# A two-layer encoder trunk on one core: splits of the dense mixer one turn earlier, another order and form of the router, another hand-over at the end

## The reference

```python
def swiglu(h, w_gate_up, w_down):
    g, u = jnp.split(h @ w_gate_up, 2, axis=-1)
    return (jax.nn.silu(g) * u) @ w_down

def moe_swiglu(h, w_router, w_gate_up, w_down):
    ...
    logits = (t @ w_router).astype(jnp.float32)
    top_val, top_idx = lax.top_k(logits, TOP_K)
    gates = jax.nn.softmax(top_val, axis=-1)
    combine = jnp.sum(jax.nn.one_hot(top_idx, N_EXPERTS, dtype=jnp.float32) * gates[..., None], axis=1)
    y = jnp.zeros_like(t)
    for e in range(N_EXPERTS):
        y = y + combine[:, e:e + 1].astype(t.dtype) * swiglu(t, w_gate_up[e], w_down[e])
    return y.reshape(B, S, D)

# in reference(), per layer l
        x = x + jnp.concatenate([y_self, y_mem], axis=-1) @ w_out[l]
        h = rmsnorm(x, ffn_norm_g[l])
        if l % 2 == 0:
            x = x + swiglu(h, w_gate_up_dense[l // 2], w_down_dense[l // 2])
        else:
            x = x + moe_swiglu(h, w_router[l // 2], w_gate_up_moe[l // 2], w_down_moe[l // 2])
    ...
    return rmsnorm(x, final_norm_g)
```

## Time and profile before

| | us |
|---|---|
| median of 3 runs | 1471.72 |
| lowest and highest | 1469.70, 1471.96 |
| profiled execution, its time | 1471.91 |
| profiled execution, its span | 1470.0 |
| PE busy | 1424.3 (97%) |
| DVE busy | 1156.0 (79%) |
| ACT busy | 949.9 (65%) |
| POOL busy | 40.0 (3%) |

### The profile page before, as it was taken

The page is one execution under the profiler, slowest core; times in us unless marked ns, Lnnn a source line. Parts: engine busy times, 40 slices in busy tenths (PEclk is TensorE's granted clock), DMA queues, the critical chain, the costliest instruction groups (busy, mean ns, idle before and its releaser), DMA issues.

```text
span 1470.0 us, 20457 instructions
## 1 busy us (share of the span) xinstructions
PE 1424.3 (97%) x7657; PEld 1210.9 (82%) x7657; DVE 1156.0 (79%) x1024; ACT 949.9 (65%) x869; POOL 40.0 (3%) x70
## 2 busy tenths in 40 slices
PE   7999999999998899999999999999999999999995
PEld 6997999998987788888888888888888888888774
DVE  6675544456776788888988888888889888988995
ACT  5445444435456577777777777777777777777673
POOL 2000000000000100000000000000000000001100
PEclk9999999999999799999999999999999999999998
DMA  9644455555533799999999999999999999999991
GB/s 309 200 130 138 148 173 172 190 190 178 172 116 114 283 374 374 381 384 367 384 379 375 392 367 376 387 368 386 385 362 389 381 371 379 371 390 358 333 348 56
DMA packets 206779, 438.38 MB, mean 298 GB/s; under 512 B 7184, under 2 KB 54288, under 8 KB 206720
## 3 DMA queue, kind: packets, MB, share of 16 engines
q1 hardware_dynamic: 202592, 423.65, 79.3%
q0 software_dynamic: 4128, 13.93, 2.7%
HBM read 431.79 MB, written 5.77 MB: 298 GB/s over the span
## 4 chain that ended last, share of the span: by engine, by line
PE 93%; DVE 4%; ACT 2%; issue 1%; DMA 0%; DVEq 0%; ACTq 0%; POOLq 0%
PE bank L1747 29%; PE bank L1749 29%; PE bank L1748 28%; PE bank L2299 2%; DVE wlo L1033 1%; ACT whi L654 1%; PE bank L1866 0%; PE bank L2225 0%; PE bank L1904 0%; PE bank L1885 0%; PE bank L1930 0%; PE bank L1871 0%; PE bank L2201 0%; DVE X L1636 0%; DVE op_lo L1103 0%
## 5 line engine op out<-in xcount | busy, mean ns | idle before, releaser
L1033 DVE TENSOR_TENSOR wlo<-raw,whi 128x2048 fp32r<-128x2048 f32 x397 | 907.1, 2290 | 178.7 <-ACT whi L654 177.4
L654 ACT CAST whi<-raw 128x2048 fp32r<-128x2048 f32 x397 | 758.1, 1914 | 213.3 <-PE bank L1749 213.3
L1747 PE MATMUL bank<-whi,op_hi 128*128 128x512 f32 (+1 forms) x1176 | 443.2, 377 | 3.2 <-DVE op_lo L1385 1.6
L1749 PE MATMUL bank<-whi,op_lo 128*128 128x512 f32 (+1 forms) x1176 | 435.5, 370 | 0.0
L1748 PE MATMUL bank<-wlo,op_hi 128*128 128x512 f32 (+1 forms) x1176 | 434.9, 370 | 0.0
L1747 PEld LDWEIGHTS bank<-whi,op_hi 128*128 128x128 f32 x1176 | 222.2, 189 | 45.2 <-DVE wlo L1033 3.9
L1749 PEld LDWEIGHTS bank<-whi,op_lo 128*128 128x128 f32 x1176 | 222.0, 189 | 38.4
L1748 PEld LDWEIGHTS bank<-wlo,op_hi 128*128 128x128 f32 x1176 | 222.3, 189 | 35.7
L1747 PE MATMUL bank<-whi,h2T_hi 128*128 128x512 f32 x544 | 214.6, 394 | 3.6 <-DVE wlo L1033 2.6
L1749 PE MATMUL bank<-whi,h2T_lo 128*128 128x512 f32 x544 | 212.5, 391 | 0.0
L1748 PE MATMUL bank<-wlo,h2T_hi 128*128 128x512 f32 x544 | 212.5, 391 | 0.0
(11 more groups left out here) (309 smaller groups left out, 800.9 us busy)
## 6 DMA issues: line engine op xcount, KB each, us to landing
raw<-in_w_gate_up_moe_dram SPq DMA_DIRECT2D x223, 1024.0 KB, 7.1
raw<-in_w_down_moe_dram SPq DMA_DIRECT2D x109, 1024.0 KB, 7.1
raw<-in_w_gate_up_dense_dram SPq DMA_DIRECT2D x22, 1024.0 KB, 5.2
raw<-in_w_down_dense_dram SPq DMA_DIRECT2D x11, 1024.0 KB, 4.9
raw<-in_w_in_a_dram SPq DMA_DIRECT2D x10, 1024.0 KB, 13.2
raw<-in_w_out_dram SPq DMA_DIRECT2D x8, 1024.0 KB, 5.0
raw<-in_w_kv_shared_dram SPq DMA_DIRECT2D x6, 1024.0 KB, 5.2
raw<-in_w_mem_kv_dram SPq DMA_DIRECT2D x4, 1024.0 KB, 6.3
```

The costliest lines, as they stand in the source:

```text
L654: a.copy(whi[:, c % SPLIT, :], src).then_inc(hi_ready, 1)
L1033: d.tensor_tensor(wlo[:, c % SPLIT, :], src, whi[:, c % SPLIT, :].bitcast(F32), ALU.subtract).then_inc(lo_ready, 1)
L1747: m.matmul(dst, sh, mh, start=start and i == 0, stop=False)
L1749: last = m.matmul(dst, sl, mh, start=False, stop=stop and i == n - 1)
```

## The change

**Dense mixer.** The split of G(j+1) moves from the start of a turn to the end of the one before, on ACT behind the split of D(j-1), on DVE ahead of `ffn_mul(j)`; G1's split comes ahead of the first silu and the first multiplication. **Router.** PE transposes the first token tile ahead of the last quarter of the last product. The logits are computed as 16 rows by 256 tokens, moved to SBUF and folded to `128x8` by two small float32 products. GpSimd multiplies X by the gain, ACT scales by the norm; the split of `hn` goes, and `gather` takes `hn` itself in plain float32, 16 products. The gates' difference is computed behind `one_hot`. **Last expert.** `add_stored` comes one tile at a time in steps 2, 3, 4 and 5. **End.** ACT starts on the first half of the last rows when PE has finished that half (`y_half`); PE spreads them into four banks without waiting for DVE's additions; ACT takes the final norm's squares piece by piece behind each addition; ACT and DVE read the flag ahead of the last expert instead of behind it; the branch of ACT and DVE stands behind these squares and additions; the output goes out in four DMAs of 256 KB. Squares are now written to `spare` tiles and not to `hn`.

The heart of the diff:

```diff
-        return 7 - int(use[4]) % 2
+        return (7, 6, 2, 3)[int(use[4])]
...
+        def load_flag(engine):
+            engine.wait_ge(route_ready, 1)
+            return engine.value_load(over_i[0:1, 0:1], min_val=0, max_val=1)
...  GpSimd
-            pool.wait_ge(hn_hi_ready, 1)
-            g.tensor_tensor(hn_lo[:, 0, :], hn[:, 0, :], hn_hi[:, 0, :].bitcast(F32), ALU.subtract).then_inc(hn_lo_ready, 1)
+            pool.wait_ge(gain_in, 16 * 3)
+            for t in range(NT):
+                pool.wait_ge(x_out, 6 + 2 * t)
+                g.tensor_tensor(hn[:, t, :], X[:, t, :], gain[:], ALU.mult).then_inc(hn_gained, 1)
...  ACT, dense mixer
+            split_hi(U_FFN + ffn_pos("G", 1))
             ffn_silu(0)
             with act.Fori(0, (FFN_STEPS - 1) // 2) as it:
                 for j in (1, 2):
-                    split_hi(U_FFN + ffn_pos("G", j), it)
                     ffn_h2_hi(j - 1, 2 * it)
                     split_hi(U_FFN + ffn_pos("U", j), it)
                     ffn_silu(j, it)
                     split_hi(U_FFN + ffn_pos("D", j - 1), it)
-            split_hi(U_FFN + FFN_UNITS - 1)
+                    split_hi(U_FFN + ffn_pos("G", j + 1), it)
...  ACT, router
+            norm_fill_hi(6, (0, 1))
             norm_sqrt(6, 0)
             sum_squares(2, x_out, 4)
-            norm_fill_hi(6)
+            norm_fill_hi(6, (2, 3))
             sum_squares(3, x_out, 4)
-            norm_sqrt(6, 1)
             for t in range(NT):
-                act.wait_ge(hn_ready, 26 + 2 * t)
-                a.copy(hn_hi[:, t, :], hn[:, t, :]).then_inc(hn_hi_ready, 1)
+                if t:
+                    norm_sqrt(6, t)
+                act.wait_ge(hn_gained, t + 1)
+                act.wait_ge(scale_ready, t + 1)
+                a.activation(hn[:, t, :], hn[:, t, :], ACT.Copy, scale=stat[:, 6, 3, t:t + 1]).then_inc(hn_ready, 2)
...  ACT, end
+                flag = None if ps else load_flag(act)
                 expert(N_EXP - 1, 0, final=True)
-                output_hi(N_EXP)
-            experts_act(0)
-            act.wait_ge(route_ready, 1)
-            flag = act.value_load(over_i[0:1, 0:1], min_val=0, max_val=1)
+            flag, output_hi = experts_act(0)
+            sqrt_table()
+            output_hi(N_EXP)
+            for q in range(4):
+                sum_squares(q, x_added, 4 + NT * 2)
             with act.If(flag == 1):
                 experts_act(1)
...  DVE, dense mixer
+            split_lo(U_FFN + ffn_pos("G", 1))
             ffn_mul(0)
...
-                    split_lo(U_FFN + ffn_pos("G", j), it)
                     ffn_h2_lo(j - 1, 2 * it)
                     split_lo(U_FFN + ffn_pos("U", j), it)
                     split_lo(U_FFN + ffn_pos("D", j - 1), it)
+                    split_lo(U_FFN + ffn_pos("G", j + 1), it)
                     ffn_mul(j, it, 2 * it)
-            split_lo(U_FFN + FFN_UNITS - 1)
...  DVE, router
             add_rows(0)
             add_rows(1)
+            add_rows(2)
             norm_mean(6, 0, 2)
-            add_rows(2)
+            norm_fill_lo(6, (0, 1))
             add_rows(3)
-            norm_fill_lo(6)
+            row_scale(0)
+            norm_fill_lo(6, (2, 3))
             norm_mean(6, 1, 2)
-            norm_scale(6, 0)
-            apply_gain(6, X, 6, 0, 0)
-            apply_gain(6, X, 6, 0, 1)
-            norm_scale(6, 1)
-            for h in range(2):
-                apply_gain(6, X, 6, 1, h)
+            dve.wait_ge(logitT_ready, 1)
+            d.tensor_copy(logT, bank[4][0:2 * N_EXP, 0:SEQ]).then_inc(logitT_out, 1)
+            row_scale(1)
             dve.wait_ge(logit_ready, 1)
-            step(d.tensor_tensor(lg[:], lg[:], sums[:, :, N_EXP:2 * N_EXP], ALU.add))
...
-            dve.wait_ge(hn_hi_ready, 2)
-            d.tensor_tensor(hn_lo[:, 1, :], hn[:, 1, :], hn_hi[:, 1, :].bitcast(F32), ALU.subtract).then_inc(hn_lo_ready, 1)
...  DVE, last expert
-                        if j in (2, 4) and final and not ps:
-                            add_stored(j // 2 - 1)
+                        if 2 <= j <= 5 and final and not ps:
+                            add_stored((j - 2) // NT, (j - 2) % NT)
...  DVE, end
-            dve.wait_ge(route_ready, 1)
-            flag = dve.value_load(over_i[0:1, 0:1], min_val=0, max_val=1)
             with dve.If(flag == 1):
                 experts_dve(1)
-            d.memset(over[:, 1:2], 0.0).then_inc(x_final, 1)
+            norm_mean(7, 0, 2)
+            norm_mean(7, 1, 2)
...  PE
+                        if between is not None and t == h == 1:
+                            between()
...
-                                last = one_pass(b[:, P * c:P * (c + 1)], hn_hi[:, t, cols], hn_lo[:, t, cols],
-                                                slot_oh[:, t, :], slot_oh[:, t, :], t == 0, t == NT - 1)
+                                last = m.matmul(b[:, P * c:P * (c + 1)], hn[:, t, cols], slot_oh[:, t, :].bitcast(F32),
+                                                start=t == 0, stop=t == NT - 1)
...
+                            if final and not ps and j == MOE_STEPS - 1 and a == 1 and h == 0:
+                                last.then_inc(y_half, 1)
...  SP
-            for t in range(NT):
-                sp.wait_ge(hn_ready, 30 + 2 * t)
-                sp.dma_start(out[0, P * t:P * (t + 1), :], hn[:, t, :]).then_inc(out_done, 16)
+            for g in range(2 * NT):
+                t, cols = g // 2, slice(512 * (g % 2), 512 * (g % 2 + 1))
+                sp.wait_ge(hn_ready, 29 + g)
+                sp.dma_start(out[0, P * t:P * (t + 1), cols], hn[:, t, cols]).then_inc(out_done, 16)
```

161 lines of the change are left out of this document (104 added, 57 removed).

## The result

The changed kernel takes 1452.10 us (median of 4 runs, 1451.89 to 1452.82), against 1471.84 for the kernel before in the same comparison: ratio 0.9869, 95% interval 0.9852 to 0.9886. The forecast was 1455.5, the range 1449.5 to 1461.5. Against 30 executions of the kernel before in a later comparison (median 1470.92, 1469.08 to 1473.11) the same median is 18.8 us less and not 19.7.

The account below looks back on a forecast made before the run. PE was taken as the limit in the experts, so gains had to come from gaps elsewhere. Terms -4.8 - 0.5 - 4.6 - 1.9 + 0.3 - 4.9 = -16.4 from 1471.9 gave 1455.5 us, range 1449.5 to 1461.5.

Parts of the forecast that it names:

- Terms 1 and 2: Dense mixer: at its start the wait for G1 and half clock go, -4.8 us; at its last step, -0.5.
- U1's tie: Dense mixer's start: U1's split ready at 178.8, PE wants it at 178.9; may cost some tenths of a us.
- Term 3: Router: gather starts 2.9 us earlier and regains full clock, DVE's chain then limits; -4.6 us, bounds -2.9 and -6.7.
- The conversion: Router: DVE's conversion of the indices, 1.25 us, ending with GpSimd's instruction, would take 0.17; 1.1 us saved.
- Term 4: Last expert: one stored tile per step removes two stalls of 1.44 us and leaves four of 0.2; -1.9 us.
- Term 5: Flag load ahead of the last expert: costs +0.3 us there, bounded by 0 and 1.5.
- Term 6: End: earlier additions 1.6, no flag load 1.0, shorter norm 1.9, smaller last DMA 0.4; -4.9 us, bounds -3 and -6.5.
- The first rival: Clock gives nothing back, port or flag costs its bound: -10, 1461 to 1463; less gain, 1459 to 1466, had 18%.
- the port's 1.0: Router: GpSimd could hold the norm's `tensor_scalar` on DVE through their shared port, costing about 1.0 us.
- The second rival: Clock holds through the router, -6.7, and the end gives -6: -21, 1450; more gain, below 1452, had 14%.
- 13 us or less behind the last output product's end: Router: where the gather's start would lie, named as a sign that the prediction is right.
- the slower turn of the loop: Dense mixer: U(j+1)'s split chain overruns its 4.4 us slack each step, kernel slower, 1475 say; slower had 4%.

Follow-up runs that it names:

- b_gather: Kernel before with only the first gather in plain float32, 16 products instead of 32, the split of `hn` still computed: 1468.62 us, ratio 0.9985.
- a_comb: Changed kernel with DVE's weights of combination cut in four pieces, put into steps 1, 2, 4 and 6 of expert 0: 1451.32 us, ratio 0.9870.
- a_hold: Changed kernel with GpSimd's second multiplication started only when the logits are in SBUF, beside the conversion of the indices: one run, 1456.06 us.
- b_flag_free: Kernel before with the flag read ahead of the last expert and DVE's wait for its last addition moved behind the branch: 1469.23 us, ratio 0.9991.

## Why the prediction was right, and where its sum was off

- **Terms 1 and 2, dense mixer: -5.3, measured -5.2, of which 0.4 came back.** Gap and half clock went, U1's tie cost nothing that can be seen, the last step's gap shrank to 0.5. What was missed is the order behind the last step: the additions' start was left to PE although a split stood ahead of them in DVE's queue.
- **Term 3, router: -4.6, measured -5.6 up to U0's second unit.** The start of the gather was 0.2 better than summed. The size that was off is the gather: 5.2 and not 5.8, since the clock came back 3.6 us into it. That size is in part the luck of one execution: in four traces with this router the clock was back 2.9 to 4.5 us into the gather, which took 4.97 to 5.71, so the forecast's 4.7 and 5.8 lie just above. The other part: the kernel before got to that unit at 503.45, 0.15 later than I took. That plain float32 products bring the clock back, which no row showed, is shown by b_gather. That DVE's chain would eat the rest is shown by the 9.35 or 9.36 behind the gather in six kernels whose gathers took 3.57 to 6.22, and by a_comb, which takes the chain apart.
- **The conversion.** Shown by a_hold. The Trainium skill ("SBUF — State Buffer", Who interferes with whom), by which GpSimd's instruction can hold the ports that such a DVE instruction needs, agrees with it. The norm's `TENSOR_SCALAR`, for which the prediction's side note gave a price of 1.0 us, lay beside GpSimd's instruction and took 0.15; the section ties it to conditions on the instruction's operands, which the note left out.
- **Term 4, stored tiles: -1.9, measured -1.7.** Four stalls of 0.34, not 0.2: the slow first product behind each stall was left out of the four, as it was of the two.
- **Term 5, flag: +0.3, measured 0.0** in both kernels that allow the comparison.
- **Term 6, end: -4.9, measured -6.0.** This is the step that was most off, and it was an overlap. Additions (E + 4.2), norm (4.15 from DVE's return to the last scaling's end, forecast 4.0) and last DMA (2.5, forecast 2.6) came as summed. The split of the 3.85 into a load of 1.0 and a branch of 2.84 was right in size (0.95 and 2.90 by the records), and the branch did stay, with 3.03. What was wrong is where the sum put it: wholly behind the last addition. It goes out 1.13 us ahead of that addition's end, and DVE is back at E + 6.1 and not at E + 7.15. Of the 1.95 us by which DVE's stretch shrank, 1.69 are the load and the wait ahead of the branch (from +0.95 to -0.74, b_flag_free), 0.39 PE's earlier spreading, and 0.13 go off, since the branch itself took longer. The move of the wait stood in no term of the sum. Against the other executions of the kernel before the gain would be 6.6 to 7.0.
- **Not in the sum:** 1.26 us up to the dense mixer and 0.2 in the experts, both within what executions of one kernel differ by.
- **Sums and signs.** The first rival's -10 comes out only with both the port's 1.0 and the flag's 1.5; with the flag alone, as listed, it is -11.1, 1460.8. The second rival's terms give -20.6, 1451.3 and not 1450. Of the signs, "13 us or less behind the last output product's end" couldn't tell: the gather began 12.4 us behind the start of the last addition in the kernel before, and 8.4 in the changed one.
- **Rivals.** The clock gave back what was taken; the slower turn of the loop didn't come (no wait of PE in the dense mixer but the last); DMA set nothing.

## What to carry to other kernels

When a stretch of idle time is removed, look for the next limit in each engine's own queue: here it was each time an instruction that had been hidden by the stretch (a split ahead of additions, the weights of combination, the other engine's branch). At a branch, read its own record: the idle stretch is the time from the branch to the next instruction, less what the engine still has in its queue when the branch goes out. So keep waits and loads from standing ahead of it, and put it where its engine, and every other that has one, is busy with earlier work or idle anyway. Where PE must stand idle ahead of work that matters, a few products that nobody reads can cost less than the half clock behind the gap.
